# Cross-attention of a two-layer stack issued between the tiles of its projections

## The chip, the core and the metric

The kernel runs on one core of a Trainium2 chip. The number that counts is the time of one execution on the device, in microseconds (us). A profiled execution gives a trace: for each engine, which instruction ran when. The engines are PE (matrix products, with PEld for its weight loads), DVE (vector work), ACT (scalar functions), POOL and SP (both here issue transfers). Each has its own instruction queue, served in order, and they meet only through semaphores.

## What is computed

The reference is a long program for 512 tokens of width 1024: two layers of recurrent mixers, each followed by a cross-attention over a memory of 256 entries and a gated feed-forward block, and then a third layer with two attentions and 32 experts. The change touches the cross-attention of the two layers, with the projection ahead of it (the mixers' output) and the one behind it:

```python
x = x + mixed @ w_mix_out
xn, mem_n = rms_norm(x, xa_g), rms_norm(mem, mem_g)
q = (xn @ wq).reshape(B, T, 4, 256)
kv = (mem_n @ wkv).reshape(B, M, 2, 4, 256); k, v = kv[:, :, 0], kv[:, :, 1]
s = einsum('bthd,bmhd->bhtm', q, k) * 256 ** -0.5
p = softmax(s, axis=-1)
o = einsum('bhtm,bmhd->bthd', p, v).reshape(B, T, 1024)
x = x + o @ wo
```

## The kernel before

Everything is fp32. Activations lie transposed, features on the 128 partitions and the 512 tokens along the row, so 1024 features are 8 blocks of 128 x 512. **A projection** (`Linear`) takes its weights in chunks of 128 x 1024. SP loads them into a ring of 4 (`weight_ring`). To keep fp32 precision at the faster `fp32r` rate, each chunk is split in a high and a low part: ACT casts the high part (`chunk_high`, L293), DVE subtracts to get the rest (`chunk_rest`, L299), both into one of two halves of `chunk_split`. The activations are split the same way (`x_high` L305 and L307, `x_rest` L313 and L315). `tile_products` (L326) then makes one output tile of 128 x 512 from 8 blocks x 3 products (high.high, high.low, low.high), 24 matmuls. `token_products` (L339) uses a chunk the other way round, for an output with tokens on the partitions; its units are half as long. A chunk's half becomes free when the tile two places earlier is done, which the semaphore `chunk_used` says. So ACT and DVE can split one chunk ahead of PE, and no more. PE waits for the split of its chunk (`chunk_taken`). Output tiles rotate over banks 0 to 3; DVE takes each out of its bank (`bank_free`).

**The order around the attention is written out by hand** in Python loops, one for each engine. `attention_in` is one stage: the tiles `mixed` (8, with `add_mixed`, L598, adding them to the residual), the memory's `keys` (8 tiles of 256 tokens, `keys_out` L602), `values` (8 units, `values_out` L607) and `queries` (8 tiles, `queries_out` L612). Two norms are made on the side: squares on ACT (L352), summed by DVE (`add_square`, L360) and PE (L370), a root on ACT (`take_roots`, L379) and a reciprocal on DVE (`invert_roots`, L387). `cross_attention` is a second stage: for each of 4 heads the scores (L1590), their row maximum (L1638), the exponential (L1625), its normalisation (L1643), the transposes of the probabilities (L1604) and their copy (L1631), the product with the values (L1612) and the copy of the result into `MIX` (L1646). `block_out` is the third: the projection `out` (8 tiles, `add_out` L861), then the feed-forward block. At the end of each stage all engines meet.

Of the kernel before, what the change touches and what calls it, by code (L numbers as in the profile page):

```python
# [24 lines left out]
ALU = mybir.AluOpType  # L25
# [123 lines left out]
def program(nc, d, out):  # L149

    ctx = ExitStack()
    with ctx:
# [103 lines left out]
        def blocks_of(name, at, n=KB):  # L256
# [5 lines left out]
                   for n, places in (("scratch", (SCR_AT + 16 * T, SCR_AT + 24 * T)),  # L262
                                     ("proj", (PROJ_AT + 12 * T, PROJ_AT + 20 * T)),
                                     ("mix", (MIX_AT, SCR_AT + 16 * T)))}
# [65 lines left out]
        def token_products(pe, lin, c, bank):  # L330

            pe.wait_ge(chunk_taken.sem, RING + lin.c0 + c + 1)
            for k in (2 * (c % 4), 2 * (c % 4) + 1):
                if c < 4 and lin.fresh:
                    pe.wait_ge(x_lo.sem, lin.x0 + k + 1)
                for tt in range(lin.tokens // P):
                    for a, b in PARTS:
                        at = ((lin.c0 + c) % 2) * KB * P + (k % 2) * T
                        mm = pe.matmul(banks[:, bank + tt, :], lin.split[b][k][:, tt * P:(tt + 1) * P],  # L339
                                       chunk_split[:, a, at:at + T], start=(k, a, b) == (0, 0, 0), stop=(k, a) == (KB - 1, 1))  # L340
            mm.then_inc(chunk_used.sem, 1)
# [82 lines left out]
        def linear_tokens(groups, x, out, place="scratch", early=None):  # L424
# [7 lines left out]
            def pe(pe):  # L432
                pe.wait_ge(bank_free.sem, f0 + 4)
                for c in range(4 * groups):
                    token_products(pe, lin, c, 4 * (c // 4 % 2))
# [29 lines left out]
        def mixers_in():  # L465
# [7 lines left out]
            def pe(pe):  # L473
                for c in range(4):
                    token_products(pe, values, c, 4)
# [59 lines left out]
        def attention_in(layer, kT, v_tok, q):  # L535


            mem, mem_gain = [PROJ[:, k // 2, M * (k % 2):M * (k % 2) + M] for k in range(KB)], [vec("mem_g", k) for k in range(KB)]
            x, gain = [H[:, k, :] for k in range(KB)], [vec(f"xa_g{layer}", k) for k in range(KB)]
            mixed = Linear(KB, x_split["scratch"])  # L540
            keys, values = Linear(KB, x_split["proj"], tokens=M), Linear(8, x_split["proj"], tokens=M, fresh=False, banked=False)
            queries = Linear(KB, x_split["scratch"])
            mem_norm = RowRoots(M, [S(k // 2)[:, 0, M * (k % 2):M * (k % 2) + M] for k in range(KB)], S(33)[:, 0, 0:M], 6,
                                S(33)[:, 0, M:M + 2])
            x_norm = RowRoots(T, [S(k)[:, 0, :] for k in range(KB)], S(32)[:, 0, :], 4)
            need_mem = f"mem{layer}"

            def pe(pe):
                for j in range(KB):
                    tile_products(pe, mixed, j)  # L550
                    if j == 4:
# [3 lines left out]
                for c in range(8):  # L555
                    token_products(pe, values, c, 4 + 2 * (c // 4))
                for j in range(KB):
                    tile_products(pe, queries, j)
                    if j == 0:
                        sum_squares(pe, x_norm)  # L560

            def act(act):
                for j in range(KB):
# [4 lines left out]
                    elif j == 2:  # L568
# [3 lines left out]
                    elif j == 3:  # L572
                        for k in range(KB):
                            square(act, mem_norm, k, mem[k])
                    elif j == 6:
                        take_roots(act, mem_norm)
                for j in range(KB):
                    chunk_high(act, keys, j)
                    if j >= 2:
                        act.wait_ge(bank_free.sem, mixed.freed(j - 2))  # L580
                        x_high(act, queries, j - 2, x[j - 2], gain[j - 2])
                for c in range(8):
                    chunk_high(act, values, c)
                    if c < 2:
                        act.wait_ge(bank_free.sem, mixed.freed(6 + c))
                        x_high(act, queries, 6 + c, x[6 + c], gain[6 + c])
                    elif c < 6:
                        for k in (2 * (c - 2), 2 * (c - 2) + 1):
                            square(act, x_norm, k, x[k])
                for j in range(KB):  # L590
                    chunk_high(act, queries, j)
                    if j == 2:
                        take_roots(act, x_norm)

            def dve(dve):
                def add_mixed(j):
# [6 lines left out]

                def values_out(g):
                    dve.wait_ge(chunk_used.sem, values.used(4 * g + 3))
                    for tt in range(2):
                        dve.tensor_scalar(v_tok[:, tt, g * T:(g + 1) * T], banks[:, 4 + 2 * g + tt, :],  # L607
                                          mem_norm.by_token[:, tt:tt + 1], None, ALU.mult)

                def queries_out(j):  # L610
                    dve.wait_ge(chunk_used.sem, queries.used(j))
                    dve.tensor_tensor(q[:, j, :], queries.bank(j), x_norm.roots, ALU.mult).then_inc(bank_free.sem, 1)  # L612

                for j in range(KB):
# [6 lines left out]
                    if j == 2:  # L621
# [3 lines left out]
                    elif j == 3:  # L625
                        for k in range(KB):
                            add_square(dve, mem_norm, k)
                    elif j == 7:
                        invert_roots(dve, mem_norm)
                for j in range(KB):  # L630
                    chunk_rest(dve, keys, j)
                    if j:
                        keys_out(j - 1)
                    else:
                        add_mixed(KB - 1)
                    if j >= 3:
                        x_rest(dve, queries, j - 3, x[j - 3], gain[j - 3])
                for c in range(8):
                    chunk_rest(dve, values, c)
                    if c == 0:  # L640
                        keys_out(KB - 1)
                    if c < 3:
                        x_rest(dve, queries, 5 + c, x[5 + c], gain[5 + c])
                    elif c < 7:
                        for k in (2 * (c - 3), 2 * (c - 3) + 1):
                            add_square(dve, x_norm, k)
                    if c == 5:
                        values_out(0)
                chunk_rest(dve, queries, 0)
                chunk_rest(dve, queries, 1)  # L650
                values_out(1)
                for j in range(2, KB):
                    chunk_rest(dve, queries, j)
                    if j == 2:
                        invert_roots(dve, x_norm)
                        queries_out(0)
                    queries_out(j - 1)
                queries_out(KB - 1)

            stages.append({"pe": pe, "act": act, "dve": dve})  # L660
# [59 lines left out]
        def block_out(layer, after=None):  # L720
# [5 lines left out]
            out = Linear(KB, x_split["proj"])  # L726
# [34 lines left out]
            def pe(pe):  # L761
                for j in range(KB):
# [34 lines left out]
            def act(act):  # L797
# [13 lines left out]
                for j in range(KB):  # L811
                    chunk_high(act, out, j)
                    if j == 0:
                        for k in range(KB):
                            x_high(act, out, k, MIX[:, k, :])
                    if j >= 2:
                        prepare(j - 2)
# [38 lines left out]
            def dve(dve):  # L856
# [24 lines left out]
                for j in range(KB):  # L881
                    chunk_rest(dve, out, j)
                    if j == 0:
                        for k in range(KB):
                            x_rest(dve, out, k, MIX[:, k, :])
                    if j:
                        add_out(j - 1)
                    if j >= 2:
                        x_rest(dve, up, j - 2, x[j - 2], gain[j - 2])
# [682 lines left out]

        def cross_attention(layer):
            kT = flat(XN[:, 0:4, :]).rearrange("p (k t) -> p k t", k=KB)
            v_tok = flat(XN[:, 4:8, :]).rearrange("p (t c) -> p t c", t=2)
            q = PROJ[:, 0:8, :]
            attention_in(layer, kT, v_tok, q)
            prob = [flat(S(n, 2)).rearrange("p (t k) -> p t k", t=TT) for n in (0, 2)]
            probT = [S(n, 2) for n in (4, 6)]
            low, total = S(8)[:, 0, 0:16], S(8)[:, 0, 16:32]  # L1580
# [1285 lines left out]
```

## Time and profile before

| | us |
|---|---|
| median of 3 timed runs | 3740.86 (3736.64 to 3741.22) |
| profiled execution, its own time | 3725.87 |
| its span in the trace | 3724.0 |
| PE busy | 3306.2 (89% of the span) |
| layer 0: last query tile taken out, first matmul of `out` | 695.85, 762.65 |
| layer 1: the same two | 1593.74, 1660.27 |

The busy time of PE is a sum over stages with quite different limits. The two attention stages are a small part of the span, and what they are limited by has to be read in their own stretch. A row of a timeline gives start, length, engine, line, operation, output<-inputs, shapes and count; in brackets is how long the engine had been idle and what ended that.

### The profile page before, as it was taken

The numbers are of one execution on the slowest core, as the hardware profiler recorded it, in microseconds if no ns is written. First come the engines' busy times: TensorE is split into PE (matmuls) and PEld (weight loads), VectorE is DVE, ScalarE is ACT, GpSimd is POOL, SyncE is SP. The second block draws the span as 40 slices with busy tenths as digits, with TensorE's granted clock in tenths as the row PEclk, the third lists the DMA queues.
The fourth block names the chain that finished last, engine by engine and source line by source line (L and its number), as shares of the span: only waits on it lengthen the run. The fifth ranks groups of instructions, "written<-read, shape, count | busy, mean of one in ns | idle before, by whom it ended". The sixth has DMA issues, their size and how long they took to land.

```text
span 3724.0 us, 42319 instructions
## 1 busy us (share of the span) xinstructions
PE 3306.2 (89%) x15690; PEld 2693.1 (72%) x15690; DVE 2375.8 (64%) x2354; ACT 1578.3 (42%) x1592; POOL 187.6 (5%) x212
## 2 busy tenths in 40 slices
PE   7868979889999847979999698858999999999996
PEld 6657968668788625857788575657888888888884
DVE  4545346357754355536773534657999999999995
ACT  2231214132223133323222212426777777777772
POOL 0000000000000000000000000000111111111110
PEclk9957989999999867989999798769999999999997
DMA  4200004124433201413443220037999999999993
GB/s 176 78 1 1 1 13 135 45 96 143 152 111 107 68 12 36 139 46 108 147 130 97 96 85 29 23 136 292 385 386 377 388 381 382 388 377 388 383 378 142
DMA packets 118822, 638.43 MB, mean 171 GB/s; under 512 B 13417, under 2 KB 13417, under 8 KB 68785
## 3 DMA queue, kind: packets, MB, share of 16 engines
q1 hardware_dynamic: 98592, 560.52, 40.3%
q0 software_dynamic: 20112, 76.24, 6.8%
q8 instruction: 86, 1.41, 0.2%
q14 instruction: 32, 0.25, 0.0%
HBM read 612.07 MB, written 24.64 MB: 171 GB/s over the span
## 4 chain that ended last, share of the span: by engine, by line
PE 71%; DVE 11%; ACT 3%; issue 1%; DMA 1%; DVEq 1%; SPq 0%; ACTq 0%; POOLq 0%
PE banks L326 25%; PE banks L2363 19%; PE banks L2380 9%; PE banks L785 7%; PE banks L339 2%; PE banks L1612 1%; PE banks L1741 1%; DVE chunk_split L299 1%; PE banks L2357 1%; PE banks L2348 1%; PE banks L2369 1%; DVEq L2667 0%; PE banks L1033 0%; DVE scratch L870 0%; DVE scratch L1657 0%
## 5 line engine op out<-in xcount | busy, mean ns | idle before, releaser
L326 PE MATMUL banks<-x_scratch,chunk_split 128*128 128x512 f32 x4032 | 934.2, 392 | 36.2 <-DVE x_scratch L313 22.5
L326 PEld LDWEIGHTS banks<-x_scratch,chunk_split 128*128 128x128 f32 x4032 | 758.8, 189 | 205.1 <-issue 47.6
L293 ACT CAST chunk_split<-weight_ring 128x1024 fp32r<-128x1024 f32 x292 | 306.3, 1049 | 1000.5 <-PE banks L326 734.8
L2363 PE MATMUL banks<-pair_split,rows 128*128 128x512 f32 x3072 | 709.8, 392 | 0.0
L2363 PEld LDWEIGHTS banks<-pair_split,rows 128*128 128x128 f32 x3072 | 578.6, 188 | 126.4
L299 DVE TENSOR_TENSOR chunk_split<-weight_ring,chunk_split 128x1024 fp32r<-128x1024 f32 x292 | 357.0, 1223 | 230.1 <-ACT chunk_split L293 221.3
L2380 PE MATMUL banks<-pair_split,hidden_t 128*128 128x512 f32 x1536 | 361.4, 394 | 6.1 <-DVE hidden_t L2475 6.1
L2380 PEld LDWEIGHTS banks<-pair_split,hidden_t 128*128 128x128 f32 x1536 | 285.4, 189 | 69.2 <-issue 6.3
L2142 DVE TENSOR_TENSOR pair_split<-mixed,pair_split 128x2048 fp32r<-128x2048 f32 x128 | 292.9, 2289 | 34.4 <-ACT pair_split L2137 34.4
L2142 DVE TENSOR_TENSOR pair_split<-scratch,pair_split 128x2048 fp32r<-128x2048 f32 x128 | 290.3, 2287 | 36.8 <-ACT pair_split L2137 36.7
L2142 DVE TENSOR_TENSOR pair_split<-weight_ring,pair_split 128x2048 fp32r<-128x2048 f32 x128 | 290.2, 2288 | 36.1 <-ACT pair_split L2137 36.1
L2137 ACT CAST pair_split<-mixed 128x2048 fp32r<-128x2048 f32 x128 | 244.9, 1914 | 65.4 <-PE banks L2363 53.4
L2137 ACT CAST pair_split<-scratch 128x2048 fp32r<-128x2048 f32 x128 | 244.1, 1907 | 60.2 <-PE banks L2363 59.6
L2137 ACT CAST pair_split<-weight_ring 128x2048 fp32r<-128x2048 f32 x128 | 241.3, 1910 | 60.0 <-PE banks L2363 52.0
L326 PE MATMUL banks<-x_proj,chunk_split 128*128 128x256 f32 (+1 forms) x768 | 140.7, 346 | 9.0 <-DVE x_proj L313 9.0
L326 PEld LDWEIGHTS banks<-x_proj,chunk_split 128*128 128x128 f32 x768 | 121.9, 193 | 29.0 <-issue 10.9
L785 PE MATMUL banks<-x_down_hi,chunk_split 128*128 128x512 f32 x448 | 141.6, 395 | 0.0
L866 DVE TENSOR_TENSOR scratch<-banks,scratch 128x512 f32<-128x512 f32 x88 | 60.7, 690 | 119.2 <-PE banks L326 119.1
L2513 POOL DMA_INDIRECT token_sums<-normed,tables x32 | 87.0, 2718 | 337.6 <-ACT normed L2426 326.8
L785 PEld LDWEIGHTS banks<-x_down_hi,chunk_split 128*128 128x128 f32 x448 | 84.2, 188 | 19.7
L326 PE MATMUL banks<-x_mix,chunk_split 128*128 128x512 f32 x384 | 89.5, 395 | 5.1 <-DVE chunk_split L299 5.1
L326 PEld LDWEIGHTS banks<-x_mix,chunk_split 128*128 128x128 f32 x384 | 72.9, 190 | 21.6 <-issue 5.5
(557 smaller groups left out, 3752.1 us busy)
## 6 DMA issues: line engine op xcount, KB each, us to landing
weight_ring<-in_weights SPq DMA_DIRECT2D x292, 512.0 KB, 3.6
mixed<-in_w SPq DMA_DIRECT2D x128, 1024.0 KB, 9.0
weight_ring<-in_w SPq DMA_DIRECT2D x128, 1024.0 KB, 7.7
scratch<-in_w SPq DMA_DIRECT2D x128, 1024.0 KB, 8.7
mixed<-in_w_ada POOLq DMA_DIRECT2D x48, 512.0 KB, 3.8
token_sums<-tables POOLq DMA_DIRECT2D x1, 2560.0 KB, 21.4
residual<-in_x POOLq DMA_DIRECT2D x4, 512.0 KB, 10.2
projected<-in_mem POOLq DMA_DIRECT2D x2, 1024.0 KB, 5.2
```

What stands on the lines that cost most here:

```text
L293: act.copy(chunk_split[:, 0, at:at + KB * P], flat(ring[:, n % RING])).then_inc(chunk_hi.sem, 1)
L299: dve.tensor_tensor(chunk_split[:, 1, at:at + KB * P], flat(ring[:, n % RING]), chunk_split[:, 0, at:at + KB * P], ALU.subtract).then_inc( ...
L326: mm = pe.matmul(lin.bank(j), chunk_split[:, a, at + k * P:at + (k + 1) * P], lin.split[b][k][:, 0:lin.tokens], start=(k, a, b) == (0, 0, ...
L339: mm = pe.matmul(banks[:, bank + tt, :], lin.split[b][k][:, tt * P:(tt + 1) * P], chunk_split[:, a, at:at + T], start=(k, a, b) == (0, 0, ...
L785: mm = pe.matmul(banks[:, DOWN_BANKS[m], :], chunk_split[:, a, at + (k % KB) * P:at + (k % KB + 1) * P], down.split[b][k], start=(k, a, b) ...
L866: L(dve.tensor_tensor(y, bank, norm.roots, ALU.mult))
L1612: mm = pe.matmul(banks[:, 6 + dv, :], v_tok[:, kt, (2 * h + dv) * P:(2 * h + dv + 1) * P], probT[h % 2][:, kt, :], start=kt == 0, stop=kt ...
L2137: act.copy(pair_split[s][:, 0, :], raw[r]).then_inc(pair_hi, 1)
L2142: dve.tensor_tensor(pair_split[s][:, 1, :], raw[r], pair_split[s][:, 0, :], ALU.subtract).then_inc(pair_lo, 1)
L2363: mm = pe.matmul(banks[:, n, :], rows[:, a, k, :], pair_split[k % SLOTS][:, b, n * T:(n + 1) * T], start=False, stop=(k, a) == (KB - 1, 1))
L2380: mm = pe.matmul(banks[:, 4 + n, :], hid_t[:, a, k, :], pair_split[c][:, b, at:at + T], start=(k, a, b) == (0, 0, 0), stop=(k, a) == (KB - ...
L2513: pool.indirect_dma_start(sums, bass.IndirectOffsetOnAxis(row_out, 0), y_tok, None, compute_op=ALU.add)\
```

## The change

The three stages become one. `attention(layer)` now returns its part of each engine's program, and `layer_end` (formerly `block_out`) runs it ahead of the rest, with no meeting of the engines between. Inside, the order is new:

- The weights come in the order mixed, keys, queries, values, out (values and queries have changed places).
- The memory is split one tile earlier (at tile 1 of `mixed`), into buffers of its own (`x_memory`). The residual is split and squared during `mixed` (`prepare`), into `x_queries`. The sum of squares of the residual, with its root and reciprocal, is made during `keys` in place of `queries`.
- The scores of heads 0, 1, 2 are issued behind query tiles 2, 4, 6, and those of head 3 behind value unit 1. Each head has its own buffers for probabilities.
- The transposes (`turn`) stand behind value units 3, 4, 6, 7. The value units write banks 0 to 3, and scores, transposes and outputs banks 4 to 7.
- The four outputs come behind the last transposes. Each is copied to `MIX`, split and used by `out` without a stage end.

```diff
-        def attention_in(layer, kT, v_tok, q):
+        def attention(layer):
...
+            prob = [flat(S(2 * h, 2)).rearrange("p (t k) -> p t k", t=TT) for h in range(4)]
+            probT = [S(16 + 2 * h, 2) for h in range(4)]
...
             def pe(pe):
...
                 for j in range(KB):
                     tile_products(pe, mixed, j)
-                    if j == 4:
+                    if j == 5:
                         sum_squares(pe, mem_norm)
                 for j in range(KB):
                     tile_products(pe, keys, j)
-                for c in range(8):
-                    token_products(pe, values, c, 4 + 2 * (c // 4))
+                    if j == 3:
+                        sum_squares(pe, x_norm)
                 for j in range(KB):
                     tile_products(pe, queries, j)
-                    if j == 0:
-                        sum_squares(pe, x_norm)
+                    if j in (2, 4, 6):
+                        scores(j // 2 - 1)
+                pe.wait_ge(bank_free.sem, queries.freed(5))
+                for c in range(8):
+                    if c == 4:
+                        pe.wait_ge(bank_free.sem, queries.freed(7))
+                    token_products(pe, values, c, value_banks[c // 4])
+                    if c == 1:
+                        scores(3)
+                    elif c in (3, 4):
+                        turn(c - 3)
+                    elif c in (6, 7):
+                        turn(c - 4)
+                for h in range(4):
+                    output(h)
...
             def dve(dve):
...
+                chunk_rest(dve, keys, 0)
+                add_mixed(KB - 1)
+                x_rest(dve, queries, 6, x[6], gain[6])
+                add_square(dve, x_norm, 6)
+                chunk_rest(dve, keys, 1)
+                invert_roots(dve, mem_norm)
+                keys_out(0)
+                x_rest(dve, queries, 7, x[7], gain[7])
+                add_square(dve, x_norm, 7)
+                for j in range(2, KB):
+                    chunk_rest(dve, keys, j)
+                    keys_out(j - 1)
+                    if j == 6:
+                        invert_roots(dve, x_norm)
                 for j in range(KB):
-                    chunk_rest(dve, keys, j)
+                    chunk_rest(dve, queries, j)
                     if j:
-                        keys_out(j - 1)
+                        queries_out(j - 1)
                     else:
-                        add_mixed(KB - 1)
...
+                    if j in (3, 5, 7):
+                        lowest((j - 3) // 2)
+                    elif j in (4, 6):
+                        shares((j - 4) // 2)
...
+                for h in range(4):
+                    mixed_out(h)
+                    if h:
+                        for k in (2 * h - 2, 2 * h - 1):
+                            x_rest(dve, out, k, MIX[:, k, :])
+                for k in (6, 7):
+                    x_rest(dve, out, k, MIX[:, k, :])
```

`lowest` is the row maximum, `shares` the normalisation, `mixed_out` the copy into `MIX`. On ACT the exponentials stand behind the high parts of the chunks for query tiles 4 and 6 and value units 0 and 3, the copies of the transposes behind those of value units 5 and 6 and of `out` tiles 0 and 1.

DVE's queue at the change from `mixed` to `keys`, layer 0. Before, L598 adds a tile to the residual, L299 splits a chunk, L387 and L389 are the memory's reciprocals and L602 takes out a key tile:

```order
L299 TENSOR_TENSOR chunk_split<-weight_ring,chunk_split 128x1024
L598 TENSOR_TENSOR residual<-residual,banks 128x512
L299 TENSOR_TENSOR chunk_split<-weight_ring,chunk_split 128x1024
L602 TENSOR_TENSOR normed<-banks,scratch 128x256
L299 TENSOR_TENSOR chunk_split<-weight_ring,chunk_split 128x1024
```

Of the changed kernel the same place, from the split of key chunk 0 (first row) to that of key chunk 2 (last row):

```order
L301 TENSOR_TENSOR chunk_split<-weight_ring,chunk_split 128x1024
L696 TENSOR_TENSOR residual<-residual,banks 128x512
L317 SCALAR_TENSOR_TENSOR x_queries_57<-residual,tables,x_queries_56 128x512
L362 TENSOR_TENSOR scratch<-scratch,normed 128x512
L301 TENSOR_TENSOR chunk_split<-weight_ring,chunk_split 128x1024
L389 RECIPROCAL scratch<-scratch 128x256
L391 RECIPROCAL scratch<-scratch 128x2
L700 TENSOR_TENSOR normed<-banks,scratch 128x256
L317 SCALAR_TENSOR_TENSOR x_queries_57<-residual,tables,x_queries_56 128x512
L362 TENSOR_TENSOR scratch<-scratch,normed 128x512
L301 TENSOR_TENSOR chunk_split<-weight_ring,chunk_split 128x1024
```

Between the splits of key chunks 0 and 2 stand two residual splits, two sums of squares and the memory's reciprocals that stood elsewhere; further on, the long reciprocal (L389, 128x512) stands right ahead of the split of key chunk 7.

PE's queue between the last projection of the attention and `out`, layer 0, before (L326 are the last query product and the first of `out`):

```order
L326 MATMUL banks<-x_scratch_50,chunk_split 128x512
L1590 MATMUL banks<-normed,projected 128x256 x16
L1604 MATMUL banks<-tables,scratch 128x128 x8
L1612 MATMUL banks<-scratch,normed 128x512 x4
L1590 MATMUL banks<-normed,projected 128x256 x8
L1604 MATMUL banks<-tables,scratch 128x128 x8
L1612 MATMUL banks<-scratch,normed 128x512 x4
L1590 MATMUL banks<-normed,projected 128x256 x8
L1604 MATMUL banks<-tables,scratch 128x128 x8
L1612 MATMUL banks<-scratch,normed 128x512 x4
L1604 MATMUL banks<-tables,scratch 128x128 x8
L1612 MATMUL banks<-scratch,normed 128x512 x4
```

Of the changed kernel what stands between the last value unit (L341) and `out` (L328):

```order
L341 MATMUL banks<-chunk_split,x_memory_58 128x512
L590 MATMUL banks<-tables,scratch 128x128 x8
L601 MATMUL banks<-scratch,normed 128x512 x16
L328 MATMUL banks<-x_proj_52,chunk_split 128x512
```

All scores and three of the four groups of transposes have moved up between tiles and units. Left here are the last transposes and the outputs.

## Rows read from the trace of the kernel before

**Rows 1.** The page: busy time of the engines
```profile
PE 3306.2 (89%) x15690; PEld 2693.1 (72%) x15690; DVE 2375.8 (64%) x2354; ACT 1578.3 (42%) x1592; POOL 187.6 (5%) x212
```

**Rows 2.** Timeline of PE, layer 0, keys to the first tiles of out
```profile
604.74 23.20 PE L326 MATMUL banks<-x_proj,chunk_split 128*128 128x256 f32 x192
627.77 16.92 PE L339 MATMUL banks<-chunk_split,x_proj 128*128 128x512 f32 x72
645.54 5.85 PE L339 MATMUL banks<-chunk_split,x_proj 128*128 128x512 f32 x24 [0.85 <-DVE chunk_split L299]
...
714.91 3.62 PE L1590 MATMUL banks<-normed,projected 128*128 128x256 f32 x16
721.17 1.09 PE L1604 MATMUL banks<-tables,scratch 128*128 128x128 f32 x8 [2.64 <-DVE scratch L1643]
...
762.65 12.73 PE L326 MATMUL banks<-x_proj,chunk_split 128*128 128x512 f32 x44 [4.56 <-DVE x_proj L313]
```

**Rows 3.** Chain that ended last, layer 0, table load of head 0, head 1: start, us, what
```profile
701.98 1.28 ACT L1625
...
716.34 1.14 DVE scratch L1638
...
717.71 1.94 ACT scratch L1625 x8
...
719.89 1.24 DVE scratch L1643
...
722.30 1.02 ACT scratch L1631
```

**Rows 4.** Timeline of PE's weight loads, end of head 0's outputs
```profile
713.63 0.19 PEld L1612 LDWEIGHTS banks<-scratch,normed 128*128 128x128 f32 x1 [0.24 <-issue]
714.05 0.19 PEld L1612 LDWEIGHTS banks<-scratch,normed 128*128 128x128 f32 x1 [0.24 <-issue]
```

**Rows 5.** Timeline of DVE: last query tiles, first out tile, layer 1's last query
```profile
690.41 0.69 DVE L612 TENSOR_TENSOR projected<-banks,scratch 128x512 f32<-128x512 f32 x1 [3.08 <-PE banks L326]
695.85 0.69 DVE L612 TENSOR_TENSOR projected<-banks,scratch 128x512 f32<-128x512 f32 x1 [4.75 <-PE banks L326]
...
770.77 0.69 DVE L861 TENSOR_TENSOR residual<-residual,banks 128x512 f32<-128x512 f32 x1 [2.92 <-PE banks L326]
...
1593.74 0.69 DVE L612 TENSOR_TENSOR projected<-banks,scratch 128x512 f32<-128x512 f32 x1 [4.75 <-PE banks L326]
```

**Rows 6.** Timeline of PE, layer 1: first matmul of out
```profile
1660.27 19.97 PE L326 MATMUL banks<-x_proj,chunk_split 128*128 128x512 f32 x75 [4.46 <-DVE x_proj L313]
```

**Rows 7.** Windows: us, PE, PEld, DVE, ACT, POOL busy, granted clock, DMA, GB/s
```profile
723.30:727.00 3.70, 3.64 (x5) 1.70 (x6) 0.00 (x0) 0.01 (x1) 0.00 (x0) 0.55 0.00 0
...
762.60:766.00 3.40, 3.35 (x8) 2.71 (x9) 3.40 (x6) 3.08 (x6) 0.00 (x0) 0.50 0.45 154
...
828.70:834.40 5.70, 5.70 (x25) 4.71 (x26) 2.26 (x3) 0.30 (x1) 0.00 (x0) 1.00 0.56 183
```

**Rows 8.** Timeline of PE, feed-forward: a stall within dense matmuls
```profile
828.68 44.23 PE L326 MATMUL banks<-x_scratch,chunk_split 128*128 128x512 f32 x192 [1.56 <-DVE chunk_split L299]
```

**Rows 9.** Timeline of DVE and ACT: single operations of the projections
```profile
600.10 1.75 DVE L387 RECIPROCAL scratch<-scratch 128x256 f32<-128x256 f32 x1
...
604.99 1.05 ACT L293 CAST chunk_split<-weight_ring 128x1024 fp32r<-128x1024 f32 x1 [4.39 <-PE banks L326]
...
606.07 1.23 DVE L299 TENSOR_TENSOR chunk_split<-weight_ring,chunk_split 128x1024 fp32r<-128x1024 f32 x1 [0.45 <-ACT chunk_split L293]
607.81 0.42 DVE L602 TENSOR_TENSOR normed<-banks,scratch 128x256 f32<-128x256 f32 x1 [0.51 <-PE banks L326]
...
613.91 0.74 DVE L315 SCALAR_TENSOR_TENSOR x_scratch<-residual,tables,x_scratch 128x512 fp32r<-128x512 f32 x1
...
635.85 0.68 DVE L360 TENSOR_TENSOR scratch<-scratch 128x512 f32<-128x512 f32 x1
...
659.14 3.35 DVE L387 RECIPROCAL scratch<-scratch 128x512 f32<-128x512 f32 x1
```

More of the change, by code:

```diff
@@ L263, in program @@
                                      ("proj", (PROJ_AT + 12 * T, PROJ_AT + 20 * T)),
-                                     ("mix", (MIX_AT, SCR_AT + 16 * T)))}
+                                     ("mix", (MIX_AT, SCR_AT + 16 * T)), ("queries", (MIX_AT, PROJ_AT + 20 * T)))}
+        x_split["memory"] = [[half[:, M * n:M * (n + 1)] for half in blocks_of(f"x_memory_{part}", PROJ_AT + (12 + 4 * part) * T, 4)
+                              for n in range(2)] for part in range(2)]
         x_split["down"] = [blocks_of("x_down_hi", XN_AT),
@@ L338, in token_products @@
                         at = ((lin.c0 + c) % 2) * KB * P + (k % 2) * T
[L339 removed]
+                        mm = pe.matmul(banks[:, into[tt], :], lin.split[b][k][:, tt * P:(tt + 1) * P],
                                        chunk_split[:, a, at:at + T], start=(k, a, b) == (0, 0, 0), stop=(k, a) == (KB - 1, 1))
@@ L648, in dve @@
                         values_out(0)
-                chunk_rest(dve, queries, 0)
-                chunk_rest(dve, queries, 1)
+                chunk_rest(dve, out, 0)
                 values_out(1)
[L652 to L660, printed above, removed]
+                chunk_rest(dve, out, 1)
@@ L662, in program @@
+                for h in range(4):
+                    mixed_out(h)
[4 more added lines that the diff above has]
+                    x_rest(dve, out, k, MIX[:, k, :])
+            return out, pe, act, dve
         ADA_GROUPS = 6
@@ L725, in block_out @@
             n_up, n_down = 2 * FF_TILES, KB * DOWN_CHUNKS
-            out = Linear(KB, x_split["proj"])
+            out, attention_pe, attention_act, attention_dve = attention(layer)
             up = Linear(n_up, x_split["scratch"])
@@ L879, in add_down @@
                     dve.tensor_tensor(x[m], x[m], banks[:, DOWN_BANKS[m], :], ALU.add).then_inc(h_ready.sem, 1)
-                for j in range(KB):
+                attention_dve(dve)
+                add_out(0)
+                for j in range(2, KB):
                     chunk_rest(dve, out, j)
[L883 to L889, printed above, removed]
+                    add_out(j - 1)
+                    x_rest(dve, up, j - 2, x[j - 2], gain[j - 2])
                     if j >= 3:
```

265 lines of the change are left out of this document (139 added, 126 removed).

## Prediction

> **What bounds the kernel now.** On the page, PE is busy for 89% of the span [rows 1], so elsewhere only fewer or denser matmuls help. The attention is the exception, and I read it in four views. The timeline of PE gives its edges in layer 0. The last query tile is taken out at 695.85 [rows 5] and `out` begins at 762.65 [rows 2]: 66.8 us, in which PE makes only scores, transposes and outputs. The chain that ended last shows why: for each head it walks maximum 1.14, exponentials 1.94, normalisation 1.24, transposes, copy 1.02 [rows 3], one engine after the other, with PE idle for 2.64 us ahead of the transposes [rows 2]. The granted clock is the third view. It is 0.55 in head 1's outputs, and 0.50 in the first matmuls of `out`, that is mostly the lower level, 1.2 GHz [rows 7]. Last come the single operations of the projections [rows 9], since these decide whether the moved work has room there.
>
> **What is removed, per layer.** (a) The stretch itself, 762.65 - 695.85 = 66.8 in layer 0 and 1660.27 - 1593.74 = 66.5 in layer 1 [rows 2, 5, 6]. Both stage ends lie in it. (b) The slow start of `out`: its first tile takes 770.77 - 762.65 = 8.1 [rows 2, 5]. A query tile at full clock takes 695.85 - 690.41 = 5.44 [rows 5]. After the change PE has been busy for over 100 us when `out` starts, so 2.7 go. (c) The wait of 0.85 ahead of a value unit [rows 2]. There the DVE had its sums of squares and the first `values_out` between two splits; now the unit has scores or transposes beside it. Together 70.3 and 70.0.
>
> **What PE keeps, and now does between tiles.** Four scores at 3.62 = 14.5, four groups of transposes at 1.09 = 4.4 [rows 2], and four outputs. These cost 0.42 a matmul pass at full clock, the distance of two weight loads [rows 4], so 8 passes are 3.4 a head, 13.7 in all. Sum 32.6. I take full clock for all, since PE has no long gap any more.
>
> **What else moves, step by step** (times on the axis of layer 0; the start of the stage and tiles 0 to 7 of `mixed` are to end at 604.9 as before). A split costs DVE 1.23, about 1.14 to the next start; the ACT part ahead of it is 1.05 [rows 9]. So a tile's split is ready 1.05 + 1.23 + 0.1 = 2.4 after its half comes free, if DVE is. A tile lasts 5.44, a key tile 23.20 / 8 = 2.9, a value unit 16.92 / 6 = 2.8 [rows 2].
>
> - `mixed`: behind each tile DVE now adds (0.69, as L861 in [rows 5]), splits a residual block (0.74), sums a square (0.68) and splits the next chunk (1.23) [rows 9], 3.3 in all. With the memory's 256-wide sums (some 0.45 each, an estimate between half and all of 0.68) it is 5.1 in the fullest tile, against 5.44. It fits, with 0.3 to spare. The memory's eight splits at tile 1, at 0.42 each (the 256-wide operation on the bank [rows 9]), 3.3 + 0.6 + 1.2 = 5.1, fit too. Cost 0; it would be 0.3 a tile if I am off.
> - `keys` has no such room. PE ends `mixed` at 604.9. DVE adds the last tile (0.6), splits residual block 6 (0.75), sums (0.7) and only then splits key chunk 1: ready at 604.9 + 2.1 + 1.2 = 608.3, while PE ended key tile 0 at 607.8. **Stall 0.5.** Then, ahead of the split of chunk 2, come the memory's reciprocals (1.75 + 0.2), a key tile out (0.34), block 7 (0.75) and its square (0.65): 3.7. That split is ready at 608.2 + 3.7 + 1.2 = 613.1, and PE has ended tile 1 at 611.1. **Stall 2.0.** Tiles 2 to 6 find DVE free. Ahead of chunk 7 stands the long reciprocal, 3.35 [rows 9]. It begins when tile 5 has been taken out (625.9), so the split ends at 625.9 + 3.4 + 1.2 = 630.5; PE ended tile 6 at 628.4. **Stall 2.1.** Sum 4.6. Queued behind these on DVE are only further splits and outputs of keys, and PE alone waits for them. In the kernel before, the long reciprocal lay under a tile of 5.44, and cost nothing.
> - `queries`: the row maximum waits on DVE for the scores, and the split of the next tile's chunk is queued behind it. Scores of head 0 end 3.62 after tile 2; maximum and scaling take 1.4 more, the split 1.2. PE is in tile 3 for 5.44 after the scores: 2.8 to spare. The normalisation waits for ACT (table load 1.28 and exponentials 1.94 [rows 3], some 3.3 after the maximum) and ends 2.2 after tile 3 ended or sooner, with the split behind it 3.4 after. Hidden by tile 4. The same holds for heads 1 and 2. Cost 0. Without that cover each head would cost up to its 1.4 + 3.3 + 1.4 = 6.1.
> - `values`, units of 2.8: unit 1's split is ready at 690.1, PE wants it at 690.6 (the tightest place). Scores 3 then give 3.6 of room, and each group of transposes 1.1. Head 3's exponentials end some 7 after its scores' start; its transposes come four units later. The copies on ACT (1.02) end before the outputs want them. Cost 0.
> - The tail: outputs alternate between banks, so a head's copy (1.2) and splits lie under the next head's 3.4. Behind the last output, the first matmuls of `out` need only blocks 0 to 3; block 4 is wanted 4 x 0.68 = 2.7 later and is ready after 1.2 + 0.7. Cost 0.
> - Transfers: 24 chunks of the same size in another order; the ring is refilled by the same rule, and the shortest spacing of chunks stays 2.8. One exponential table load per layer, as before. The one for SiLU in layer 0 moves to the head of the stage, where ACT idles. Cost 0.
>
> **Sum.** 70.3 - 32.6 - 4.6 = 33.1 in layer 0, and 32.8 in layer 1: 65.9 in all. Against the profiled execution, 3725.9 - 65.9 = 3660.0. The median of the runs shown is 15.0 above that execution. Nothing in this change acts on that difference, so the timed median should be 3740.9 - 65.9 = 3675.
>
> **Rivals.**
>
> *The clock falls at the stalls in `keys`.* Three new stalls, of up to 2.1. A fall costs about what the start of `out` showed, 2.7 [rows 5]. For it: after gaps of 2.64 and 1.1 with little work between, the clock was at 0.55 [rows 2, 7]. Against it: after a stall of 1.56 amid dense matmuls [rows 8] it stayed at 1.00 [rows 7]. Mine are as dense on both sides and only somewhat longer. If both long stalls bring it down in both layers, 4 x 2.7 = 10.8: 3686. The Trainium skill (TensorE: Matmul & The Clock Gate, section HAM oscillation — how this bites in real kernels) says that waits between bursts of matmuls can put PE back to 1.2 GHz each time, so that the next burst pays again. The trace agrees for the gaps between heads, and not for the 1.56 one. By that rule it would be the 3686. Chance 0.15.
>
> *The stalls in `keys` are smaller or absent*, because the DVE operations overlap more than I take. Gain up to 9.2: down to 3666. Chance 0.12.
>
> *The heads' chain is only partly hidden*: each head's maximum, exponentials and normalisation hold back a split, because DVE's queue is in order. Full price 6.1 a head by the step above, 49 in all: 3724, a gain of half a percent. Anything between is possible; the room of 2.8 behind head 0's scores speaks against more than a fraction. Chance 0.08, mostly near 3690 to 3700.
>
> *Slower than before: every split of the sixteen query tiles and value units comes late.* The half of a chunk comes free only as the previous tile begins, and a split then takes 2.4. If waits on DVE push each one wholly out of its cover, 16 x 2.4 = 38.4 against the 33 gained: 5 lost per layer, 3751. It decides from 33 / 16 = 2.1 a tile. Against it, query tiles leave 3.0 of free time each [rows 5, 9]. Chance 0.03.
>
> *The change does not do what it says*: PE still meets a barrier between attention and `out`. The order of PE's queue shows no stage end there, and outputs wait only on copies. Chance 0.02, 3741.
>
> **The numbers.** My forecast, 3669 to 3682, has 0.6; the likeliest value is 3675. The range of 3663 to 3692 takes in absent stalls, the fallen clock, and the 5 or so by which the runs shown differ; it leaves out the two last rivals and most of the third. A measurement of this kernel can tell about 0.2%, 7.5 us. Faster by more than that: 0.95. Within: 0.02. Slower: 0.03.
>
> **What would show it.** PE busy in the stretch from first key tile to first `out` tile with no gap over 3; gaps of about 0.5, 2.0 and 2.1 within the key tiles, each ended by a split (L301), the last preceded by L389 on DVE. Matmul groups of scores at 3.62, transposes at 1.09, outputs at 3.4 each; granted clock 1.00 throughout; from the first matmul of `keys` to the first `out` tile taken out about 133 in place of 770.77 - 604.74 = 166.0 [rows 2, 5]. It would be wrong if gaps stood ahead of query tiles or value units, if the clock were 0.5 within `keys`, or if the first `out` tile still took 8.

## The result, and the profile after

The changed kernel takes 3667.5 us, median of four runs (3662.7 to 3678.5), beside 3738.8 of the kernel before (3736.6 to 3741.2). The ratio is 0.9824 with an interval of 0.9803 to 0.9844, a gain of 1.8%. The forecast was 3675, with a range of 3663 to 3692. By the ratio the saving is 0.0176 x 3738.8 = 66, with 58 to 74 from its interval; by the two medians it is 71. The sum was 65.9. That close agreement is partly luck: inside the traces the attention gives back 63.9, and terms that were missed are offset by terms that were costed too high. The profiled execution took 3670.56 with a span of 3668.7.

The page of after, busy time of the engines. The work is that of before, PE's busy time is 13 us shorter:
```profile
PE 3292.8 (90%) x15690; PEld 2694.6 (73%) x15690; DVE 2373.9 (65%) x2354; ACT 1579.4 (43%) x1593; POOL 185.8 (5%) x212
```

The timeline of PE in layer 0, from the first keys to `out` (columns as in [rows 2]; numbers in brackets are idle time ahead, and what ended it):
```profile
614.80 3.04 PE L328 MATMUL banks<-x_memory,chunk_split 128*128 128x256 f32 x24
618.36 3.09 PE L328 MATMUL banks<-x_memory,chunk_split 128*128 128x256 f32 x24 [0.52 <-DVE chunk_split L301]
623.08 5.93 PE L328 MATMUL banks<-x_memory,chunk_split 128*128 128x256 f32 x48 [1.63 <-DVE chunk_split L301]
...
629.30 9.10 PE L328 MATMUL banks<-x_memory,chunk_split 128*128 128x256 f32 x72
640.69 4.60 PE L328 MATMUL banks<-x_memory,chunk_split 128*128 128x256 f32 x24 [2.29 <-DVE chunk_split L301]
645.13 16.96 PE L328 MATMUL banks<-x_queries,chunk_split 128*128 128x512 f32 x72
661.93 3.62 PE L578 MATMUL banks<-normed,projected 128*128 128x256 f32 x16
...
729.43 13.90 PE L601 MATMUL banks<-scratch,normed 128*128 128x512 f32 x32
742.77 37.51 PE L328 MATMUL banks<-x_proj,chunk_split 128*128 128x512 f32 x159
```
There is no bracket between 640.69 and the tiles of `out`: the gaps of 2.64 ahead of transposes and of 4.56 ahead of `out` [rows 2] are gone. The only waits left are three in `keys`: 0.52, 1.63 and 2.29, where the prediction had 0.5, 2.0 and 2.1.

Ahead of the first late split (616.98) DVE adds the last mixed tile, splits a residual block and adds its square, from 615.00 on. The timeline of DVE has this split, the two other late ones, a reciprocal ahead of each of these, and where the first tile of `out` is taken out:
```profile
616.98 1.23 DVE L301 TENSOR_TENSOR chunk_split<-weight_ring,chunk_split 128x1024 fp32r<-128x1024 f32 x1
618.13 1.75 DVE L389 RECIPROCAL scratch<-scratch 128x256 f32<-128x256 f32 x1
...
621.71 1.22 DVE L301 TENSOR_TENSOR chunk_split<-weight_ring,chunk_split 128x1024 fp32r<-128x1024 f32 x1
...
635.94 3.34 DVE L389 RECIPROCAL scratch<-scratch 128x512 f32<-128x512 f32 x1
639.32 1.23 DVE L301 TENSOR_TENSOR chunk_split<-weight_ring,chunk_split 128x1024 fp32r<-128x1024 f32 x1
...
748.94 0.69 DVE L993 TENSOR_TENSOR residual<-residual,banks 128x512 f32<-128x512 f32 x1 [1.94 <-PE banks L328]
```
The chain that ended last (start, us, what; each piece begins where the one before it ends) now runs through PE's matmuls without leaving it from 640.69 to the end of the outputs, in place of the walk over DVE and ACT of [rows 3]:
```profile
623.08 5.93 PE banks L328 x48
...
629.87 5.71 PE banks L328 x48
...
635.60 0.42 DVE normed L700
636.02 3.27 DVE scratch L389
639.29 0.02 issue
639.32 1.24 DVE chunk_split L301
640.55 0.14 issue
640.69 21.40 PE banks L328 x96
662.09 3.45 PE banks L578 x16
665.54 11.19 PE banks L328 x48
...
714.96 0.87 PE banks L590 x8
...
729.60 13.74 PE banks L601 x32
743.33 46.70 PE banks L328 x201
```
Windows (columns as in [rows 7]) give the granted clock around the stalls, on 4 stretches: behind the 0.52, behind the 1.63, behind the 2.29, and in the first tile of `out`:
```profile
618.40:621.40 3.00, 3.00 (x24) 2.83 (x24) 2.93 (x5) 0.58 (x1) 0.00 (x0) 1.00 0.56 169
623.00:626.00 3.00, 2.92 (x25) 2.96 (x25) 1.39 (x2) 0.00 (x0) 0.00 (x0) 1.00 0.56 182
...
640.70:645.20 4.50, 4.50 (x25) 4.50 (x26) 1.31 (x2) 0.00 (x0) 0.00 (x0) 0.62 0.63 207
...
743.40:748.90 5.50, 5.50 (x25) 4.49 (x24) 3.60 (x5) 1.14 (x2) 1.61 (x4) 1.00 0.05 9
```
So `out` starts at full clock, where [rows 7] had 0.50. But the third stall was followed by 0.62, and its key tile takes 4.44 (640.69 to 645.13) in place of 2.9.

**One length for all comparisons.** From the first matmul of the attention stage to the first `out` tile taken out I write S. Before it is 770.77 - 557.87 = 212.9 in layer 0 and 212.6 in layer 1. After, it is 748.94 - 568.24 = 180.7, and 180.9 in layer 1. The saving is 32.2 and 31.7, 63.9 in all; 65.9 were forecast. S doesn't move with what runs ahead of the stage, which differs by up to 18 us between executions (last section). That is most of why the spans differ by only 3724.0 - 3668.7 = 55.3: the profiled execution of before began its layer-0 attention at 557.87, and that of after at 568.24.

### The profile page after: what moved, and what is told of

Its sections match the earlier page's. It is cut to its first block, busy times and chain, and to the rows that moved or that the text cites. A ratio compares the mean times of both kernels' runs of the same rounds, so it can differ in the third digit from the quotient of the medians.

```text
span 3668.7 us, 42312 instructions
## 1 busy us (share of the span) xinstructions
PE 3292.8 (90%) x15690; PEld 2694.6 (73%) x15690; DVE 2373.9 (65%) x2354; ACT 1579.4 (43%) x1593; POOL 185.8 (5%) x212
## 3 DMA queue, kind: packets, MB, share of 16 engines
q8 instruction: 86, 1.41, 0.2%
## 4 chain that ended last, share of the span: by engine, by line
PE 72%; DVE 10%; ACT 2%; issue 1%; DMA 1%; DVEq 1%; SPq 0%; ACTq 0%; POOLq 0%
PE banks L328 24%; PE banks L2415 19%; PE banks L2432 9%; PE banks L920 7%; PE banks L341 2%; PE banks L1793 1%; DVE chunk_split L301 1%; PE banks L2409 1%; PE banks L2400 1%; PE banks L2421 1%; PE banks L578 1%; PE banks L601 1%; DVEq L2717 0%; PE banks L1162 0%; DVE scratch L1002 0%
## 5 line engine op out<-in xcount | busy, mean ns | idle before, releaser
L328 PE MATMUL banks<-x_scratch,chunk_split 128*128 128x512 f32 x3648 | 845.2, 392 | 36.7 <-DVE x_scratch L315 22.7
L328 PEld LDWEIGHTS banks<-x_scratch,chunk_split 128*128 128x128 f32 x3648 | 686.3, 189 | 189.7 <-issue 47.1
L328 PE MATMUL banks<-x_mix,chunk_split 128*128 128x512 f32 x384 | 89.6, 395 | 5.1 <-DVE chunk_split L301 5.1
L328 PE MATMUL banks<-x_queries,chunk_split 128*128 128x512 f32 x384 | 91.8, 398 | 0.0
L328 PE MATMUL banks<-x_proj,chunk_split 128*128 128x512 f32 x384 | 90.4, 397 | 0.0
L328 PEld LDWEIGHTS banks<-x_mix,chunk_split 128*128 128x128 f32 x384 | 73.0, 191 | 21.7 <-issue 5.5
```

The source lines that it names most:

```text
L328: mm = pe.matmul(lin.bank(j), chunk_split[:, a, at + k * P:at + (k + 1) * P], lin.split[b][k][:, 0:lin.tokens], start=(k, a, b) == (0, 0, ...
```

## Experiments

**Is the third stall what the long reciprocal costs, and the low clock with it?** The 3.34 us operation is moved from the keys to under a query tile:
```diff
 # dve, loop over keys
-                    if j == 6:
-                        invert_roots(dve, x_norm)
 # dve, loop over queries, behind chunk_rest(dve, queries, j)
+                    if j == 1:
+                        invert_roots(dve, x_norm)
```


> One edit to the changed kernel: the long reciprocal (128x512, 3.35) no longer stands on DVE ahead of the split of key chunk 7, but behind that of query chunk 1, under a query tile. Measure: S, from the first matmul of the attention stage to the first out tile taken out, 180.7 in layer 0 of the changed kernel (212.9 before). Theory (the stall of 2.29 ahead of key tile 7 is this reciprocal, and it brings the granted clock down in the tile behind it, 4.6 in place of 2.9): both go, S falls by 4.0 to 176.7. Rival (the slow key tile 7 has nothing to do with the stall): only 2.3 go, S 178.4. Rival (DVE is simply full and the stall moves to a query tile): S unchanged, a gap of 2 ahead of query tile 1 or 2.

S is 741.91 - 565.41 = 176.5, and 177.1 in layer 1: shorter by 4.2 and 3.8. One run took 3664.0. Timeline of PE, key tiles of layer 0:
```profile
615.45 3.12 PE L328 MATMUL banks<-x_memory,chunk_split 128*128 128x256 f32 x24 [0.52 <-DVE chunk_split L301]
620.17 5.92 PE L328 MATMUL banks<-x_memory,chunk_split 128*128 128x256 f32 x48 [1.60 <-DVE chunk_split L301]
...
626.39 11.96 PE L328 MATMUL banks<-x_memory,chunk_split 128*128 128x256 f32 x96
638.18 16.89 PE L328 MATMUL banks<-x_queries,chunk_split 128*128 128x512 f32 x72
```
Four key tiles now run in one piece. The operation is as long as before; only its cover changed. What went is the stall, 2.3, and beside it 1.9 in layer 0 and 1.5 in layer 1, about the 1.6 that the lowered clock had added. The granted clock is 1.00 over these four tiles, and also over the query tile that now has the reciprocal beside it (640.6 to 644.1). So the operation itself doesn't lower the clock; what it had done was to hold PE up. The stall and the fall went together, and no run here has the one without the other.

**All three stalls taken out.** As above, and the DVE's operations between the last `mixed` tile and key tile 3 are spread over four splits:
```diff
 # dve
+                invert_roots(dve, mem_norm)
                 chunk_rest(dve, keys, 0)
                 add_mixed(KB - 1)
                 x_rest(dve, queries, 6, x[6], gain[6])
-                add_square(dve, x_norm, 6)
                 chunk_rest(dve, keys, 1)
-                invert_roots(dve, mem_norm)
+                add_square(dve, x_norm, 6)
                 keys_out(0)
+                chunk_rest(dve, keys, 2)
                 x_rest(dve, queries, 7, x[7], gain[7])
+                keys_out(1)
+                chunk_rest(dve, keys, 3)
                 add_square(dve, x_norm, 7)
-                for j in range(2, KB):
+                keys_out(2)
+                for j in range(4, KB):
```
(PE's sum of x's squares goes from key tile 3 to 5, ACT's roots from 5 to 7.)

> The edit of the run above, and also: the memory's reciprocals (1.75 and 0.17) moved from between key chunks 1 and 2 to ahead of key chunk 0, the sum of square 6 behind the split of key chunk 1, residual block 7 and its square behind those of chunks 2 and 3, and the sum of squares on PE two key tiles later. Theory: each of the three stalls (0.52, 1.63, 2.29) is set by what stands ahead of a split in DVE's queue, so all three go, and with them the slow clock in key tile 7: S = 180.7 - 4.4 - 1.7 = 174.6, two layers 12 less, a timed median near 3655 and a ratio to the kernel before of 0.977 to 0.979. Rival (DVE is too full in the key tiles of 2.9 for any order): stalls of more than 1 in sum remain, S 177 or more.

Timeline of PE: six key tiles without a bracket.
```profile
619.11 17.33 PE L328 MATMUL banks<-x_memory,chunk_split 128*128 128x256 f32 x144
636.28 1.02 PE L372 MATMUL banks<-scratch,tables 128*128 128x512 f32 x2
636.73 6.26 PE L328 MATMUL banks<-x_memory,chunk_split 128*128 128x256 f32 x48
```
S is 746.60 - 572.25 = 174.4, and 174.6, shorter than the changed kernel's by 6.3 a layer. The median is 3656.4, ratio 0.9776 (0.9755 to 0.9797) to before. This version beats both kernels: 81 us less than before by the medians. It also says what the stalls cost in full: 4.4 of waiting, 1.6 of low clock, and 0.4 for two tiles behind the shorter waits. In the chain above two key tiles right behind a wait take 5.93 and two within an unbroken run 5.71, and the one behind the 0.52 takes 3.09 where an unbroken one takes 2.9.

**The stage end kept.** The same order of work, but the attention is a stage of its own, so that `out` starts behind the barrier:
```diff
+            stages.append({"pe": attention_pe, "act": attention_act, "dve": attention_dve})
 # in the stage behind it
-                attention_pe(pe)
-                attention_act(act)
-                attention_dve(dve)
```


> One edit to the changed kernel: a stage end, where all engines meet, stands again between the attention and the projection out; the interleaving is kept. Theory (the hidden chains of the heads are the gain, the missing stage end is a small part): out begins when its last block is split, some 3.8 after the last output, and maybe with a first tile at the lower clock, 2.7: S between 184.5 and 187.5. Rival (the stage ends and the late, slow start of out were a large share of the 32): S 195 or more.

S is 755.68 - 569.14 = 186.5, and 186.4: longer by 5.8 and 5.5; one run 3682.1. Timeline of PE, with DVEq the sequencer of DVE:
```profile
730.65 13.90 PE L601 MATMUL banks<-scratch,normed 128*128 128x512 f32 x32
748.32 46.30 PE L328 MATMUL banks<-x_proj,chunk_split 128*128 128x512 f32 x192 [3.77 <-DVEq L2716]
```
The barrier costs 3.8 of waiting and makes the first tile of `out` 755.68 - 748.32 = 7.4 in place of 5.6 (granted clock 0.79 in it), the rest. Letting the outputs run into `out` is thus worth 11.3 us of the 64.

**The heads left open.** The scores, the exponentials and the transposes are taken out from between the tiles and put, head by head, behind the last value unit, in the new stage without a barrier and with the new buffers. Scores 2 and 3 wait for the copy of an output:
```diff
 # pe, behind the eight value units
-                for h in range(4):
-                    output(h)
+                scores(0)
+                for h in range(4):
+                    if h < 3:
+                        scores(h + 1)
+                    turn(h)
+                    output(h)
 # act, with chunk_high(act, out, 0) and (out, 1) ahead
+                for h in range(4):
+                    exponential(h)
+                    turned_out(h)
 # dve
                 for h in range(4):
+                    lowest(h)
+                    shares(h)
                     mixed_out(h)
```


> One part of the change undone: no stage end, weights, norms and splits in the new order, but scores, transposes and outputs of the four heads stand one head behind the other behind the last value unit, as before the change, with the chain of maximum, exponentials, normalisation and copy open between them; the splits for out come behind the last head. Theory (hiding these chains is the gain): S returns to 205 to 213, the time to 3715 to 3735, a ratio to the kernel before of 0.993 to 0.999. Rival (what counted was the meeting of engines and the earlier norms): S stays below 195, ratio below 0.990.

S is 787.33 - 574.49 = 212.8, and 212.8; the median of ten runs is 3738.9, ratio 0.9999 (0.9985 to 1.0014). The whole gain is gone; the ratio is slightly above the 0.993 to 0.999 that I had expected. Timeline of PE, the heads:
```profile
727.47 1.09 PE L586 MATMUL banks<-tables,scratch 128*128 128x128 f32 x8 [1.50 <-DVE scratch L708]
729.66 5.25 PE L595 MATMUL banks<-scratch,normed 128*128 128x512 f32 x8 [1.10 <-ACT scratch L632]
736.32 3.69 PE L578 MATMUL banks<-normed,projected 128*128 128x256 f32 x16 [1.41 <-DVE mixed L713]
...
768.23 1.97 PE L586 MATMUL banks<-tables,scratch 128*128 128x128 f32 x8 [6.09 <-DVE scratch L708]
771.29 6.62 PE L595 MATMUL banks<-scratch,normed 128*128 128x512 f32 x8 [1.10 <-ACT scratch L632]
779.92 20.39 PE L328 MATMUL banks<-x_proj,chunk_split 128*128 128x512 f32 x80 [2.01 <-DVE x_proj L315]
```
These are the gaps of the kernel before again, 6.09 and 1.10 to the digit, and the outputs of 5.3 to 6.6 in place of 3.4. So it is the place between the tiles that hides them. Without it, what the new stage gives back is eaten. From the first score to `out` it takes 779.92 - 718.89 = 61.0, where before took 762.65 - 696.64 = 66.0; the start of the stage and of `out` and the value units give another 2.6. But the keys are longer by 6.4, with the same stalls (0.52, 1.63, 2.29), and the query tiles by 1.2. The copy that scores 2 and 3 now wait for (1.41) costs nothing: outputs of heads 0 and 1 start 743.20 - 729.66 = 13.54 apart, and 13.56 before.

**Why are the query tiles slower?** From 665.54 the chain has two of them in 11.19, 5.60 each, against 5.44 [rows 5]; nothing waits inside, and the clock is 1.00 over query tiles in both kernels. (Of the changed one the window is 645.4 to 651.0.) The change reads the split residual from other buffers. The run above already speaks for these: with no score between its eight query tiles, they are 5.60 apart as well. First, before's order with the high half in the mixed buffer and the low half where the high one was:
```diff
-            queries = Linear(KB, x_split["scratch"])
+            queries = Linear(KB, x_split["mix"])
```


> The kernel before, with one edit: the split residual that the query tiles read lies in the mixed buffer (high part) and in scratch blocks 16 to 23 (low part), in place of scratch blocks 16 to 23 and 24 to 31. A query tile took 5.44 before and takes 5.58 in the changed kernel, where the split lies in the mixed and the projected buffer; nobody foresaw that. Theory (where the moving operand lies sets the pace): 5.58 or near it here too, S up by 1.1 to 214.0. Rival (what runs beside the tile sets it: the scores' operations, the transfers of the new order): 5.44 here, S 212.9.

The tiles take 5.49 (680.44 to 685.93, ends by DVE), between what either theory said, and S, 782.30 - 569.57 = 212.7, is no longer than before's. By itself that settled nothing.

Next, high and low half exchanged, on top of the kernel without stalls:
```diff
-("queries", (MIX_AT, PROJ_AT + 20 * T))
+("queries", (PROJ_AT + 20 * T, MIX_AT))
```


> The kernel without stalls in the key tiles (S 174.4), with one edit: the high and the low part of the split residual change places, high in the projected buffer and low in the mixed one. The high part is read by two of three products. If one of the two buffers alone is slow, a query tile moves from 5.58 by a third of the excess over 5.44, to 5.53 or 5.63, and S by up to 0.4. If any place outside the scratch is slow, nothing changes: 5.58.

S is 743.94 - 569.62 = 174.3, and 174.6, tiles 5.53 to 5.60: no difference. Which half lies where doesn't matter.

Last, the order of before with the buffers of the changed kernel, exactly, for queries and memory:
```diff
-                                     ("mix", (MIX_AT, SCR_AT + 16 * T)))}
+                                     ("mix", (MIX_AT, SCR_AT + 16 * T)), ("queries", (MIX_AT, PROJ_AT + 20 * T)))}
...
-            queries = Linear(KB, x_split["scratch"])
+            queries = Linear(KB, x_split["queries"])
```


> The kernel before, order untouched, with the query tiles' split residual exactly where the changed kernel has it (high part in the mixed buffer, low part in projected blocks 20 to 27) and the memory's split in the changed kernel's buffers. With the high part in the mixed buffer and the low one in scratch a query tile took 5.49 (5.44 before, 5.58 in the changed kernel). Theory (the place of the moving operand, each part with its share): 5.58 here. Rival (the order of the changed kernel, scores and their operations beside the tiles, gives the rest): 5.49 or less here.

Timeline of DVE, where query tiles are taken out:
```profile
673.10 0.69 DVE L614 TENSOR_TENSOR projected<-banks,scratch 128x512 f32<-128x512 f32 x1 [3.21 <-PE banks L328]
678.68 0.69 DVE L614 TENSOR_TENSOR projected<-banks,scratch 128x512 f32<-128x512 f32 x1 [3.21 <-PE banks L328]
```
They are 5.58 apart, with the scores nowhere near: the buffers alone make the tiles slower, 8 x 0.14 = 1.1 in layer 0. The granted clock is no cause. These are windows over the query tiles, before's first:
```profile
657.20:695.80 38.60, 38.60 (x170) 31.44 (x168) 15.46 (x14) 6.62 (x7) 0.00 (x0) 1.00 0.26 82
```
```profile
655.80:695.40 39.60, 39.58 (x170) 31.60 (x168) 15.46 (x14) 6.66 (x7) 0.00 (x0) 1.00 0.27 80
```
S stays at 769.26 - 556.41 = 212.9 all the same in layer 0. The queries' part is longer by 1.05, but the transposes of head 0 take 1.10 where before's took 1.97, at a granted clock of 1.00 and 0.50 (these two rows are windows over them, before's first):
```profile
706.70:708.70 2.00, 1.97 (x8) 1.57 (x8) 0.00 (x0) 0.00 (x0) 0.00 (x0) 0.50 0.00 0
```
```profile
706.30:707.40 1.10, 1.09 (x8) 0.85 (x8) 0.00 (x0) 0.00 (x0) 0.00 (x0) 1.00 0.00 0
```
In layer 1 of the same execution S is 1670.26 - 1454.30 = 216.0, longer than before's by 3.3. The query tiles are 5.60 apart there, 1.3 more in all, and most of the rest is clock: the outputs of head 0 take 6.73 at 0.54 (before 5.18 at 0.70), the transposes of head 1 take 1.89 at 0.54 (before 1.10 at 1.00). With the heads open, S thus moves by up to 3 us with where the clock falls.

The three runs on the buffers were timed once each: 3737.6, 3659.1 and 3730.8 us, the last beside a single run of before at 3725.8.

Why a buffer's place acts on the pace of a matmul stays open.

**The changed kernel once more**, unedited, beside nine further runs of before:

> The changed kernel as it is, timed again on one chip beside the kernel before, for a narrower interval. Theory (two layers at 32 each): ratio 0.981 to 0.984, S 180.7. It also shows again how far the stretch ahead of the attention differs between executions: the first matmul of the stage came at 557.9 in the profile of before and at 565 to 574 in the five since. If that is the granted clock of the unchanged scan stage (0.86 from 500 to 540 us in the one, 0.51 to 0.56 in the others), a start near 568 goes with a clock near 0.55 here, and one near 558 with 0.86.

The median of five runs is 3670.4, ratio 0.9823 (0.9802 to 0.9844); S is 750.27 - 569.35 = 180.9, and 181.0. The four lengths S of the changed kernel agree within 0.3, so for its variants steps of 1 us in S mean something; for kernels with open heads they don't (216.0 above). The stage starts at 569.35, with a clock of 0.50 from 500 to 540 us, where some 0.55 was expected.

## Why the prediction was right, and where its terms were off

Its mechanism held: the stretch of 66.8 between the last query tile and `out` went, PE kept its own work, and the stalls came where DVE's queue was said to be too full. Term by term, for layer 0:

- *Removed, 70.3, in truth 70.5.* The stretch of 66.8 went whole. Put back, the open heads take the whole 32 with them (heads left open). Of the slow first tile 2.5 went where 2.7 was said: `out`'s first tile now takes 748.94 - 743.33 = 5.6. With the barrier left in, 1.8 of them came back. The eight value units take 22.3 in the chain in place of 23.5, so 1.2 went where 0.85 was said.
- *Kept, 32.6, in truth 31.0.* Scores take 3.45 each in the chain, not 3.62; transposes 0.87, not 1.09; outputs 13.74 in all, as said (13.7). A group's duration in [rows 2] runs to the end of its last matmul, and the tile behind it starts earlier: scores 0 last from 661.93 to 665.55, and the next query tile begins at 665.19. Over-costed by 0.7 and 0.9.
- *Stalls in `keys`, 4.6, in truth 4.4*, in the places named, ended by the split, the last behind L389. From the first key tile to the first `out` tile taken out it is 748.94 - 614.80 = 134.1, with about 133 forecast.
- *Clock falls at the stalls.* This was a rival with a chance of 0.15, at 2.7 for each of two stalls. It happened at one: behind 2.29 the clock was 0.62 and the tile lost 1.6; behind 1.63, as behind the 1.56 of [rows 8], it stayed at 1.00. So one of the prediction's own signs of being wrong, a low clock within `keys`, came for one tile a layer. The step that failed is the sentence "Mine are as dense on both sides and only somewhat longer": somewhat longer was enough. The Trainium skill (TensorE: Matmul & The Clock Gate, section HAM oscillation — how this bites in real kernels) has waits between bursts of matmuls paid for again each time (its example has longer waits); the trace agrees for the 2.29, not for the 1.63.
- *Query tiles, 5.44, in truth 5.57 to 5.60.* The prediction took a tile's length as a property of its matmuls. It missed 1.1. The buffers do it, by the last of the three runs on them.
- *Key tiles behind a wait* take 0.2 more than 2.9, beside the wait (5.93 for two against 5.71 in the chain). The prediction had nothing for this: 0.4 for the two shorter stalls.
- *Cost 0* for `mixed`, queries, values, tail and transfers held: no gap is recorded in any of them, in the tightest place (unit 1's split) neither.

The missed costs are 1.6 + 1.1 + 0.4 = 3.1. Against them stand 0.2 more removed, 1.6 less kept, 0.2 less of stalls, and a first stretch (to the keys) shorter by 46.87 - 46.56 = 0.3, which is no gain of the change: in its second profile that stretch is 46.8 again. That leaves 3.1 - 2.3 = 0.8. S is 180.7, and 212.9 - 33.1 = 179.8 was forecast: 0.9, the same within rounding.

The step from saving to time was that the timed median of before lies above its profiled execution by something the change doesn't touch. That held: the attention of that execution began 8 to 17 us sooner than in eight of the nine others, in unchanged code (last section).

## What to carry to other kernels

A chain that walks over three engines costs little when each of its links lies under a dense tile of matmuls that doesn't need it; with the same work and buffers but the heads left open, none of the gain was left. Before such a move, add up for every tile what the in-order vector queue has ahead of its next split: a key tile of 2.9 us with a split of 1.2 had no room for a reciprocal of 1.8 or 3.3 beside DVE's other work there; a query tile of 5.6 had, for the 3.3. Count for a stall what may follow it in granted clock, and take durations from a chain rather than from single groups where the next work follows without a gap.

## What the runs showed that I had not expected

**The clock of the scan stage, ahead of the attention, differs between executions.** Windows at 500 to 540 us, columns as in [rows 7]; these are before, after, and before's order with the new buffers:
```profile
500.00:540.00 40.00, 29.68 (x564) 24.68 (x564) 14.37 (x23) 3.19 (x2) 0.56 (x1) 0.86 0.08 28
```
```profile
500.00:540.00 40.00, 36.55 (x534) 31.26 (x530) 11.64 (x20) 0.00 (x0) 0.56 (x1) 0.52 0.08 28
```
```profile
500.00:540.00 40.00, 29.41 (x529) 24.35 (x525) 13.85 (x21) 3.48 (x3) 0.56 (x1) 0.84 0.08 28
```
At 0.86 and 0.84 the attention begins at 557.9 and 556.4; in the other eight profiled executions, at 0.50 to 0.56, between 565.4 and 574.5. The spans differ by 8.6 less than S alone would have it (63.9 - 55.3), and the profiled execution of before begins its attention 10.4 sooner than that of after, in unchanged code. That the timed runs differ for the same reason is argued, not shown. Their mean clocks fit: of 15 further runs of before, the two quickest (3723.8 and 3725.1) have 0.919 and 0.918, the five of 3740 or more 0.913 to 0.915. But a mean over a run doesn't say in which stage. What decides which it is stays open.

**The pace of dense matmuls depends on the buffer of the moving operand**: 24 of them take 5.44 or 5.49, or 5.57 to 5.60, at a granted clock of 1.00 where a window was read (before, changed, and before's order with the new buffers).

**A stall of 2.29 lowers the clock, one of 1.63 doesn't**, between matmuls equally dense, in each of the changed kernel's two layers (0.62 and 0.61 behind the longer one) and again in its second profile (0.60 in layer 0). No run has the 2.29 without the 1.63 some 18 us ahead of it, and none a wait between the two lengths, so what decides it stays open.
